# RWKV chunks with the state's sums issued in parts, and a mixture of experts with shorter ranks, idle products, three buffers for extra weights and reordered loads

## What is computed

```python
def step(state, inp):                       # RWKV7, 8 heads of 64, over 512 tokens
    r_t, w_t, k_t, v_t, a_t, b_t = inp
    sa = einsum('bhvk,bhk->bhv', state, a_t)
    state = state * w_t + sa[..., None] * b_t + v_t[..., None] * k_t
    return state, einsum('bhvk,bhk->bhv', state, r_t)

out = zeros_like(t)                         # 32 experts, D_EXPERT = 256, top 2
for e in range(N_EXPERTS):
    he = silu(t @ w1e[e]) * (t @ w3e[e])
    out = out + cw[:, e:e + 1] * (he @ w2e[e])
x = x + gt2 * out
return modulate(rmsnorm(x, g_final), shf, scf)
```

## Time and profile before

| | us |
|---|---|
| three runs, median (lowest, highest) | 2633.89 (2633.48, 2634.75) |
| the profiled execution, its own time | 2638.19 |
| its span, first to last instruction | 2636.3 |
| chunks stage, about | 1875.4 to 2017 |
| router, from its first idle products to the barrier | 2226.7 to 2270.6 |
| experts' loop | 2277.2 to 2589.0 |
| final combine and store | 2589.0 to 2636.3 |

### The profile page before, as it was taken

How to read it: one execution, slowest core, us unless ns; L and a number is a source line. 1 busy time by engine, 2 the same in 40 slices (tenths; PEclk the granted TensorE clock), 3 DMA queues, 4 the chain that set the end, 5 groups by cost and what they waited for, 6 DMA issues and landing times. The chain is left out here.

```text
span 2636.3 us, 38832 instructions
## 1 busy us (share of the span) xinstructions
PE 2485.2 (94%) x15328; PEld 1851.8 (70%) x15328; DVE 1150.0 (44%) x1584; ACT 950.7 (36%) x1384; POOL 999.5 (38%) x495
## 2 busy tenths in 40 slices
PE   8999999999999999999999999999898999599996
PEld 5777787788877688778778877676686776333334
DVE  5543523566553623432456654434754414311113
ACT  5543532544433434252444442344323214111112
POOL 5231522444377422351444447642224422323330
PEclk9999999999999999999999999999999999799998
DMA  3111322222266210321232236321001215699993
GB/s 134 72 49 54 107 96 80 97 90 89 75 231 214 81 65 32 112 96 64 80 112 95 90 112 235 137 97 71 2 4 50 81 63 208 232 391 346 364 352 106
DMA packets 76282, 333.88 MB, mean 127 GB/s; under 512 B 17114, under 2 KB 21210, under 8 KB 51802
## 3 DMA queue, kind: packets, MB, share of 16 engines
q1 hardware_dynamic: 62336, 313.98, 33.5%
q0 software_dynamic: 13824, 18.19, 2.0%
HBM read 372.67 MB, written 16.78 MB: 148 GB/s over the span
## 5 line engine op out<-in xcount | busy, mean ns | idle before, releaser
L227 PE MATMUL bank<-dense_s_hi,dense_w_hi 128*128 128x512 f32 x672 | 267.1, 397 | 12.8 <-POOL dense_w_lo L715 6.9
L228 PE MATMUL bank<-dense_s_lo,dense_w_hi 128*128 128x512 f32 x672 | 261.8, 390 | 0.0
L229 PE MATMUL bank<-dense_s_hi,dense_w_lo 128*128 128x512 f32 x672 | 261.8, 390 | 0.0
L715 POOL TENSOR_TENSOR dense_w_lo<-weights,dense_w_hi 128x1024 fp32r<-128x1024 f32 x77 | 199.6, 2592 | 94.4 <-ACT dense_w_hi L684 90.4
L1596 DVE TENSOR_TENSOR hidden<-up_y 128x512 f32 x44 | 158.1, 3594 | 64.6 <-ACT up_y L1560 64.0
L229 PE MATMUL bank<-xn_r,weights_r 128*128 128x512 f32 x448 | 176.0, 393 | 0.0
L2057 DVE SCALAR_TENSOR_TENSOR xn<-mix,xn 128x1024 f32<-128x1024 f32 x64 | 114.2, 1785 | 114.5 <-DMA mix<-in_modulation 108.6
L227 PEld LDWEIGHTS bank<-dense_s_hi,dense_w_hi 128*128 128x128 f32 x672 | 126.0, 188 | 53.6 <-POOL dense_w_lo L715 15.3
L1573 POOL TENSOR_TENSOR up_w_lo<-weights,up_w_hi 128x2048 fp32r<-128x2048 f32 x22 | 101.5, 4615 | 126.9 <-ACT up_w_hi L1548 126.9
L229 PEld LDWEIGHTS bank<-dense_s_hi,dense_w_lo 128*128 128x128 f32 x672 | 126.1, 188 | 26.7
L227 PE MATMUL bank<-xn_r,mix_r 128*128 128x512 f32 x352 | 140.7, 400 | 2.8 <-POOL up_xn_lo_r L363 2.6
(11 more groups left out here) (758 smaller groups left out, 6253.9 us busy)
## 6 DMA issues: line engine op xcount, KB each, us to landing
weights<-in_w_up SPq DMA_DIRECT2D x44, 1024.0 KB, 4.8
mix<-in_modulation SPq DMA_DIRECT2D x64, 512.0 KB, 5.0
weights<-in_w_xattn SPq DMA_DIRECT2D x24, 1024.0 KB, 5.0
weights<-in_experts_up SPq DMA_DIRECT2D x24, 1024.0 KB, 11.9
moe_weights<-in_experts_up SPq DMA_DIRECT2D x24, 1024.0 KB, 14.1
weights<-in_w_down SPq DMA_DIRECT2D x44, 512.0 KB, 3.8
rec_rkv<-in_experts_up SPq DMA_DIRECT2D x16, 1024.0 KB, 10.5
weights<-in_w_attn SPq DMA_DIRECT2D x8, 1536.0 KB, 6.4
```

What stands on the lines that cost most here:

```text
L227: nc.tensor.matmul(out, left.hi, right.hi, start=first, stop=False)
L228: nc.tensor.matmul(out, left.hi, right.lo, start=False, stop=False)
L229: return nc.tensor.matmul(out, left.lo, right.hi, start=False, stop=last)
L715: nc.gpsimd.tensor_tensor(w[b].lo[:, :], units.rows(b, 0, D, 0, D), w[b].hi[:, :], ALU.subtract).then_inc(w_split, 1)
```

## The change

Gates and chunks. ACT runs one Exp on a column nobody needs before the last four copies of the gates stage. PE starts the chunks stage with 10 idle products. The sums are issued in parts, one pass over all pairs for each: values and state of chunk 0's `rhs` before the last level's second half, parts that do not need `U` while ACT copies. Chunk 1's `M` is made before its `MT` at level 0. Chunk 0 keeps banks 6 and 5 for state and output, chunk 1 gets 2 and 3.

Router. Five wider matmuls make ranks and counts instead of 14, and 10, 14 and 8 idle products are put into PE's list. Only the first gather stays in the stage; three go behind the stage change.

Experts. 16 idle products before `turn(0)` and 28 before `turn_tile(0)`; three buffers for extra up halves, used in turn; on POOL the eight diagonal products stand behind the first extra loads; on SP the up loads of a step stand before the down loads of the step before it; ACT scales six of eight column groups.

```diff
+                    act.wait_ge(low_ready, 3)
+                    nc.scalar.activation(low[:, 0:1], gate_low[:, 0:1], ACT.Exp)
...
+            w.s_bank, w.y_bank = ((6, 5), (2, 3))[p]
...
+                for p, w in enumerate(chunks):
+                    for first in ((True, False) if p == 0 else (False, True)):
...
+            def part(bank, left, right, place=None):
+                for n in range(PAIRS):
+                    for h in both:
+                        mm = nc.tensor.matmul(g.bank[bank][h, n * C:(n + 1) * C], left(h, n), right(h, n),
+                                              start=(place == OPENS and n == 0), stop=(place == CLOSES), skip_group_check=True)
+                return mm
...
+            idle_products(g, 3, 10)
...
+                    if l == LEVELS - 1:
+                        pe.wait_ge(chunks[1].tokens_read, 2 * i + 2)
+                        after(pe, s_ready, 2 * i)
+                        values_part(7, chunks[0].Mk, chunks[0])
+                        state_part(7, chunks[0], chunks[0].ars[i % 2], S[0]).then_inc(chunks[0].rhs_done, 1)
...
+                product(4, lambda h, n: first.MT[h, n, :], lambda h, n: first.rhs[h, n, :]).then_inc(first.u_done, 1)
+                output_part(first, i, S[0], STATE)
+                output_part(first, i, S[0], VALUES)
+                token_part(first, 1, first.vs, OPENS)
+                pe.wait_ge(first.u_ready, i + 1)
+                token_part(first, 0, first.U, CLOSES).then_inc(first.s_done, 1)
+                output_part(first, i, S[0], UPDATES).then_inc(first.y_done, 1)
...
+            idle_products(g, 6, 10)
             pe.wait_ge(chosen, 1)
...
+            nc.tensor.matmul(g.bank[1][:, 0:TT * EXPERTS], earlier[:, :], both[:, :, :].rearrange("p t e -> p (t e)"),
+                             start=True, stop=False, skip_group_check=True)
+            for s in range(TT):
+                behind = g.bank[1][:, (s + 1) * EXPERTS:(TT + 1) * EXPERTS].rearrange("p (t e) -> p t e", e=EXPERTS)
+                mm = nc.tensor.matmul(behind, g.ones[:, :], both[:, s, :].unsqueeze(1).broadcast_to([P, TT - s, EXPERTS]),
+                                      start=False, stop=(s == TT - 1), skip_group_check=True)
...
-            for n in range(ROWS_AHEAD):
-                moe.gather(nc.gpsimd, n)
+            moe.gather(nc.gpsimd, 0)
...
+            for n in range(main_step[EXPERTS - 5] + 2):
+                for e in range(4, EXPERTS):
+                    if main_step[e - 4] == n:
+                        sp.wait_ge(up_done, n + 1)
+                        moe.load_up(sp, e)
+                for e in range(4, EXPERTS):
+                    if main_step[e - 4] == n - 1:
+                        sp.wait_ge(down_done, 2 * (n - 1) + 2)
+                        moe.load_down(sp, e)
...
+                    if s == 0 and o > 1:
+                        pool.wait_ge(up_done, more_step[o - 2] + 1)
+                    if s == 1 and o > 0:
+                        pool.wait_ge(up_half_done, more_step[o - 1] + 1)
...
+            idle_products(g, 7, 16)
             turn(0)
...
+            idle_products(g, 7, 28)
             turn_tile(0)
...
-                for k in range(KT // 2):
+                for k in range(BY_SCALAR):
```

More of the change, by code:

```diff
@@ L2555, in _ @@
                     act.wait_ge(w.y_done, i + 1)
-                    nc.scalar.activation(now(rw.y, i, p), wide((5, 3)[p]), ACT.Copy).then_inc(w.y_ready, 1)
+                    nc.scalar.activation(now(rw.y, i, p), wide(w.y_bank), ACT.Copy).then_inc(w.y_ready, 1)
         @block.gpsimd
@@ new lines, in _ @@
+                first, second = chunks
+                pe.wait_ge(first.rhs_ready, i + 1)
+                pe.wait_ge(first.inverse_step, steps * (i + 1))
+                product(4, lambda h, n: first.MT[h, n, :], lambda h, n: first.rhs[h, n, :]).then_inc(first.u_done, 1)
[4 more added lines that the diff above has]
+                token_part(first, 0, first.U, CLOSES).then_inc(first.s_done, 1)
@@ new lines, in _ @@
+                output_part(first, i, S[0], UPDATES).then_inc(first.y_done, 1)
+                values_part(7, second.Mk, second)
+                pe.wait_ge(second.inverse_step, steps * (i + 1))
+                token_part(second, 1, second.vs, OPENS)
+                pe.wait_ge(s_ready, 2 * i + 1)
+                state_part(7, second, second.ars[i % 2], S[1]).then_inc(second.rhs_done, 1)
+                output_part(second, i, S[1], STATE)
+                pe.wait_ge(second.rhs_ready, i + 1)
@@ L2713, in stage_finish_merge @@
+                product(4, lambda h, n: second.MT[h, n, :], lambda h, n: second.rhs[h, n, :]).then_inc(second.u_done, 1)
+                output_part(second, i, S[1], VALUES)
+                pe.wait_ge(second.u_ready, i + 1)
+                token_part(second, 0, second.U, CLOSES).then_inc(second.s_done, 1)
+                output_part(second, i, S[1], UPDATES).then_inc(second.y_done, 1)
 def stage_finish_merge(g, rec, rw, units, coming):
@@ L3044, in _ @@
                     mm.then_inc(logits_done, 1)
+            idle_products(g, 6, 10)
             pe.wait_ge(chosen, 1)
-            for t in range(TT):
-                for s in range(t + 1):
-                    nc.tensor.matmul(g.bank[1][:, t * EXPERTS:(t + 1) * EXPERTS], (earlier if s == t else g.ones)[:, :],
-                                     both[:, s, :], start=(s == 0), stop=(s == t))
-            for t in range(TT):
-                mm = nc.tensor.matmul(g.bank[1][:, TT * EXPERTS:(TT + 1) * EXPERTS], g.ones[:, :], both[:, t, :],
-                                      start=(t == 0), stop=(t == TT - 1))
+            nc.tensor.matmul(g.bank[1][:, 0:TT * EXPERTS], earlier[:, :], both[:, :, :].rearrange("p t e -> p (t e)"),
[4 more added lines that the diff above has]
+                                      start=False, stop=(s == TT - 1), skip_group_check=True)
             mm.then_inc(counted, 1)
+            idle_products(g, 6, 14)
             for n in range(2 * TT):
@@ L3188, in stage_experts @@
         rows_step, more_rows = sem("rows_step"), sem("more_rows")
-        more_up_ready, more_down_ready = ([sem(f"more_{what}_ready{i}") for i in range(2)] for what in ("up", "down"))
+        more_up_ready, more_down_ready = ([sem(f"more_{what}_ready{i}") for i in range(n)] for what, n in (("up", 3), ("down", 2)))
         up_half_done = sem("up_half_done")
@@ L3197, in stage_experts @@
         which, row = g.memn[:, 2, 0:MORE], g.memn[:, 2, MORE:2 * MORE]
-        more_ups = [sb(f"more_up{s}", [P, moe.UP])[:, :] for s in range(2)]
+        more_ups = [sb(f"more_up{s}", [P, moe.UP])[:, :] for s in range(3)]
         xt = [g.mix[:, 4 + 2 * i:6 + 2 * i, :].rearrange("p a (k n) -> p (a k) n", n=P) for i in range(2)]
@@ L3257, in _ @@
                 load_more_down(o)
+            for c in range(2):
+                for t in range(TT):
+                    nc.gpsimd.tensor_scalar(diagonal[c][t], g.ident[:, :], moe.weight[:, c, t:t + 1], None, ALU.mult).then_inc(diagonals, 1)
             for n in range(STEPS):
@@ L3299, in up @@
                         more = more_at[place]
-                        weights.append(more_ups)
+                        weights.append([more_ups[(2 * more + s) % 3] for s in range(2)])
                 for k in range(KT):
                     if k % 4 == 0 and more is not None:
-                        pe.wait_ge(more_up_ready[k // 4], 16 * more + 16)
+                        q = 2 * more + k // 4
+                        pe.wait_ge(more_up_ready[q % 3], 16 * (q // 3) + 16)
                     for half, w in zip(halves, weights):
@@ L3485, in affine @@
                 dve.wait_ge(scaled, t + 1)
-                for k in range(KT // 2, KT):
+                for k in range(BY_SCALAR, KT):
                     ins = nc.vector.tensor_scalar(y_of[t][:, k, :], y_of[t][:, k, :], g.gains[:, 2, k:k + 1], g.mod[:, 48 + k:49 + k],
```

87 lines of the change are left out of this document (36 added, 51 removed).

## The result

| | before | after |
|---|---|---|
| median of 15 runs, us | 2633.88 (2631.34 to 2637.23) | 2637.67 (2633.37 to 2642.36) |
| ratio, 95% interval | | 1.0017 (1.0010 to 1.0025) |
| span of the profiled execution, us | 2636.3 | 2640.5 |

The change made the kernel 0.17% slower, where a gain was forecast: 2637.67 us and not 2592, outside the range of 2583 to 2610. Yet most of its parts did what they were to do. They bring the experts' first up product 18.9 us forward (2277.16 to 2258.22), and the experts' loop gives all of it back and 5 us more.

What follows compares the result with a forecast made beforehand. The prediction took PE, busy 94% of the span, to set the time, losing to half clock, short waits and late transfers. Its terms summed to 42.1 us, from 2633.89 to a median of 2592 us, range 2583 to 2610.

Steps and rivals of the forecast that it cites:

- Step 1: Gates and chunks: moving the Exp table load ahead of the last four gates copies gains 1.3 us.
- step 2: Chunks' start: ten idle products give the first round full clock, gaining 2.2 us (bounds 0 and 2.5).
- step 7: Experts' start: earlier first up product, full clock for the first two; gain 3.0 us (bounds -1 and 3.6).
- Steps 3 and 4: Chunks: sums in parts close PE's gaps, 10.0 us; chunk 1's `M` before `MT` ends a wait, 2.0 us.
- the rival by which the parts open new gaps: Chunks: PE's list puts new waits where old ones were, so 3 us instead of 12; 2601; chance 8%.
- Steps 5 and 6: Router: fewer rank products gain 4.3 us, three gathers behind the stage change 3.9; barrier moves 8.2 us.
- Step 8: Experts' loop: reordered main loads bring expert 6's up load in time; gain 6.5 us (bounds 2 and 8).
- Step 9: Experts' loop: third buffer lets extra tiles' halves leave 3.5 us earlier; gain 8.5 us (bounds 3 and 10.3).
- Step 10: Kernel's end: 28 idle products gain 0.5 us (bounds 0 and 1.5); six column groups on ACT lose 0.1 us.
- Transfers bind the early loop: Experts' first steps: no transfer margin, so steps 8 and 9 give 5 us instead of 15; 2602; chance 17%.
- Slower: the clock falls: Experts' loop: more work brings half clock, up to 12 us a step; five steps give 2652; chance 2%.
- The idle products do not hold the clock: Chunks' and experts' start: steps 2 and 7 lose 5 us; 2597; chance 6%.

Runs made afterwards that it cites:

- after_early_extra: Changed kernel with POOL issuing half 0 of an extra tile one step sooner and half 1 ahead of gather and scatter; 2600.61 us, ratio 0.9865.
- chunks_no_idle: Kernel before with gates and chunks changed, but without the ten idle products at the chunks' start; 2622.11 us, ratio 0.9954.
- chunks_alone: Kernel before with only the gates and chunks changes, including the ten idle products; 2621.64 us, ratio 0.9949.
- before_new_loads: Kernel before with only the new order of the main loads; 2655.98 us, ratio 1.0080.
- router_alone: Kernel before with only the router changed and three gathers moved behind the stage change; 2629.83 us, ratio 0.9973.
- early_extra_no_idle: after_early_extra without any of the change's idle products; 2607.42 us, ratio 0.9891.
- after_neither: Changed kernel with the old order of the main loads and the two old buffers put back; 2613.58 us, ratio 0.9912.

## Why the prediction was wrong

- **What bounds the kernel:** right as to the places. Wrong in one number that was used as a reserve: 248 us of transfer against 288 of PE says what the loop can reach on average, and `after_early_extra` (296.9 us) comes near. It says nothing of when a given load lands.
- **Step 1 (Exp, 1.3) and step 2 (idle products, 2.2):** right in kind, about half in size. The gap fell by 0.7 us. The first round's part up to the first L2607 takes 8.11 us before, 7.35 in `chunks_no_idle` and 5.77 in `chunks_alone`; of these 1.6 us between the last two, 1.1 are left at the merge stage. The unchanged stage took 7.39 there in `before_new_loads`, so 0.7 us of the 8.11 may be scatter. Ten idle products last 2.47 us at a granted clock of 1.00, not the 1.3 that I gave them (see step 7). I had taken the whole table load for part of the chain, but DVE's own work runs beside it, and DVE waited for ACT only 0.85 us, as its timeline in the kernel before shows:

```profile
1877.48 0.42 DVE L2584 TENSOR_TENSOR weights<-rec_gelu_gate,weights 128x256 f32<-128x256 f32 x1 [0.85 <-ACT weights L2524]
```

  In the new place, too, the load ends where ACT's next operation begins (1871.33 and 1871.34). The kernel before has no gap there either: its load of 1875.43 takes 1.28 us, and ACT's next operation starts at 1876.73.
- **Steps 3 and 4 (12.0):** right. From the chunks' first product to the merge stage 138.7 us before, 126.1 in `chunks_no_idle`: 12.5 less, of which 0.8 belong to the clock of the first round, so 11.8. None of the copies' waits of the earlier trace rows is left among PE's longest in the chunks; the rival by which the parts open new gaps is out.
- **Steps 5 and 6 (8.2):** right, 7.6 in `router_alone` and 8.7 in the trace between the rank products and the barrier. No gather waited for DVE: the three that moved take 1.00 us each (2251.05 to 2254.67), beside its row computation (2250.04 to 2253.87).
- **Step 7 (3.0): failed.** I gave sixteen idle products 2.1 to 4.3 us; they took 6.41, at a granted clock of 0.57 (2250.04 to 2256.45). It was a misreading of the earlier trace rows: "x12" there are twelve records, and a product of this kind leaves two (ten products are x20, sixteen x32 above), so twelve products would take 3.2 us and not 1.60. The same misreading stands in steps 2, 5 and 10, where it cost nothing: ten take 2.4 to 2.5 us, twenty-eight take 6.52 and still end before the rows land. `turn(0)` stands behind them, while DVE was free after 3.8 us. They cost 3.6 us of start and give back about as much in clock and in transfers that are late anyway. Nor was the clock full as forecast: `up(0)` takes 7.09 us from its first matmul's start to its last one's end instead of 8.41 (granted 1.00), but `up(1)` 8.78, as much as before (granted 0.81). The part on DVE was right. In the kernel before, DVE's part of `xt` starts 5.8 us after the barrier. The small operation is the one of 1.73 us at 2272.78; it runs beside POOL's two memsets, which end at 2274.49, and the same operation behind them takes 0.29 and 0.30 us:

```profile
2270.91 3.58 POOL L3249 MEMSET experts_more_up<- 128x2048 f32 x2 [3.55 <-POOLq L2977]
2274.97 0.29 DVE L3451 TENSOR_SCALAR memn<-memn,vecs 128x16 f32<-128x16 f32 x1
2275.79 0.30 DVE L3451 TENSOR_SCALAR memn<-memn,vecs 128x16 f32<-128x16 f32 x1
2276.37 0.69 DVE L3431 COPY mix<-bank 128x512 f32<-128x512 f32 x1
```

  `before_new_loads`, `chunks_alone` and `chunks_no_idle`, which have a memset at that place too, show 1.73 us again. In the changed kernel the memsets start at 2254.67, after DVE's last small operation, and the three take 0.33, 0.29 and 0.29 us; in the other eleven traces with the memsets that late they take 0.29 to 0.33. By what means a memset beside it would cost DVE this time was not shown. The whole step was worth nothing measurable.
- **Step 8 (6.5): the term that failed most.** Its own gain came: expert 6 was in time, 4.4 and 0.9 us of waits and their clock went, and against the old order with early extra loads it is worth 8 us. The step counted what must land by `up(4)` and stopped there; it never asked what else stands in the same engines from then on, every three steps. Measured by itself it costs 18.8 us. A loss was in none of its bounds (2 and 8).
- **Step 9 (8.5): failed in its first sentence,** "Both halves of an extra tile leave 3.5 us earlier". Half 0 left at the same distance from the up product as before (5.3 us), since POOL reaches it only behind scatter, down load and gather; half 1 left 1.3 us earlier. The buffer that the third one made free was not what half 0 waited for last. And the landing time of 7.6 us was carried over as a constant, while step 8 changed the traffic that made it.
- **Step 10 (0.4):** small, as said. From the last down product to the end 47.9 us before, 46.7 after.
- **Between chunks and router,** where nothing was changed, the trace of after loses 3.4 us of the 15.2 again, in windows with clocks of 0.91 and 0.83, where the kernel before shows 1.00 in the same stretches. From the merge stage's first product to the last of L227 the traces with the old chunks take 206.3 (before), 207.4 (`before_new_loads`) and 207.7 us (`router_alone`), those with the new ones from 206.4 (`chunks_alone`) to 209.8 (`early_extra_no_idle`), with 209.7 in after. The two groups overlap, so this can be scatter from run to run; what sets it is open. Of the 15.2 us, 0.7 stood already ahead of the chunks (PE's last group of the gates stage starts at 1870.09 instead of 1870.83).
- **The rivals.** "Transfers bind the early loop" (17%) had the right engines and the wrong place and size: it took 10 us off the gain (5 instead of 15), by the first seven steps, where 30 us of waits over the whole loop came. The sign for it, more than 5 us of DMA waits in those seven steps, did appear: two waits, 11.3 us. Its counter-argument, holes of 0.6 to 0.8 in the DMA share just where PE waited, was read as spare room; the orders of loads above speak for the opposite, that such holes let the extra loads land in 7.6 us. "Slower: the clock falls" (2%) had the symptom, a clock of 0.94 in the loop, as a cause; it is the consequence of the waits: 0.99 in `after_early_extra`, where all idle products are kept and nearly all waits are gone. As to "The idle products do not hold the clock" (6%), the clock was higher with them: the chunks' first 8 us are granted 1.00 with the ten and 0.79 without, `up(0)` 1.00 behind the sixteen, and 0.50 in its first 3 us without; step 7 failed all the same, by their length. The 4%, that the moved gathers wait for DVE, did not come (1.00 us each). No rival let a change to one queue delay another's loads, and so 0.96 for faster was far too sure.

The account closes within its intervals: 15.3 for the chunks, 7.6 for the router and about 1 for the rest make 23.9 us, and `after_neither` has 23.7 (23.2 by its ratio). The new order of the loads, with the third buffer, took back 1.05% (0.9912 to 1.0017), 27.7 us. So of the 46 us between the forecast gain of 42.1 and the measured loss of 3.8, steps 8 and 9 are 42.7 (15.0 forecast, 27.7 lost), and the 3.0 of step 7 are about the size of the rest.

## What to carry to other kernels

In this kernel a load that was issued at the last moment lived on the silence of the other queue. Before you move transfers forward on one queue, list for each late-issued load of the other queues what is issued in the 10 us ahead of it and behind it until its landing, for every period of the loop and not only for the step with the wait that you want to remove; the loop's mean of 368 GB/s did not show it here. And a further buffer helps only if the issue moves too: look up in the issuing engine's own list what stands in front of it.

## What the hardware showed that I had not expected

- An extra up load beyond the first three tiles moves nearly no bytes. This is an estimate: 18.19 MB pass on POOL's queue, of which gathers and scatters of 1024 rows of 4 KB are 8.4 and three tiles of 3 MB (in binary units) 9.4. Yet where PE waited for one, it landed 9.7 to 12.5 us after its issue in the changed kernel, and 7 to 10 before. In the later periods its time followed the other queue's traffic and not its own size.
- Spreading a burst made it worse: the same bytes, 2 MB of them 5 us later, raised the waits from 30.1 to 44.9 us.
- What the empty place in a queue was worth: the old order of the loads, which left SP waiting for a down product, beat one that issued each load as soon as its buffer was free, by 18.8 us in the same kernel.
